# Fetching u and v rows of an expert pick with one indirect DMA from side-by-side tables

## The chip, the cores and the metric

The kernel runs on one core of a Trainium2 chip. A core has a matrix engine (TensorE, PE in the profile; PEld is its weight load), a vector engine (VectorE, DVE), a scalar engine (ScalarE, ACT), GpSimd (POOL), a queue engine (SyncE, SP), and 16 DMA engines that all queues share. The engines run their own instruction streams in order and wait for each other through semaphores. The metric is the device time of one execution in microseconds (us); lower is better.

## The reference

Two blocks follow each other, in float32, on 256 tokens of width 1024. The first is a hybrid mixer (gated linear attention beside a state-space scan) and a feed-forward layer of very many small experts; the second is a retention layer and a stick-breaking attention layer. The change touches the experts alone:

```python
def peer_ffn(h, w_q, sub_keys, u_tab, v_tab):      # T = 256 tokens, 8 heads, 128 x 128 experts
    q = (hb @ w_q).reshape(n, PEER_HEADS, 2, PEER_HALF)
    s = jnp.einsum('nhid,hikd->nhik', q, sub_keys)
    s_top, i_top = lax.top_k(s, PEER_TOPK)                                # 16 of 128, twice per head
    cand = s_top[:, :, 0, :, None] + s_top[:, :, 1, None, :]
    cand_idx = i_top[:, :, 0, :, None] * PEER_N_KEYS + i_top[:, :, 1, None, :]
    best, pos = lax.top_k(cand.reshape(n, PEER_HEADS, PEER_TOPK * PEER_TOPK), PEER_TOPK)
    idx = jnp.take_along_axis(cand_idx.reshape(n, PEER_HEADS, -1), pos, axis=-1)
    w = jax.nn.softmax(best, axis=-1)
    u = jnp.take(u_tab, idx, axis=0)                                      # rows of 1024 floats
    act = jax.nn.gelu(jnp.einsum('nhkd,nd->nhk', u, hb))
    out = jnp.einsum('nhk,nhkd->nd', w * act, jnp.take(v_tab, idx, axis=0))
```

So each token takes 8 x 16 = 128 experts, and for each a row of `u_tab` and a row of `v_tab`, 4096 bytes each.

## The kernel before, in words

Tokens lie on the 128 partitions, in two tiles i = 0, 1. One "pick" m is one expert for each of 128 tokens: m // 16 is the pair n of head and token tile, m % 16 the rank of the expert. There are 256 picks. A pick needs one u row and one v row per partition, 2 x 512 KB.

All weights come as a stream of 512 KB chunks on SP's queue (`load`, L186) into four `raw` buffers. `do_split` (L192) makes of each chunk a high part `whi` (ACT) and a low part `wlo` (DVE), five buffers each; `triple` (L233) multiplies with three matmuls. `XH` and `XL` hold the two parts of the activations. A side job is a generator in `sides`; `side_step` runs a piece of it between the chunks of the stream, so its instructions fall between the chunks' in program order, and `side_all` runs what is left.

The expert stage is the `stream_T` of `peer_w_q` at L1122 (16 chunks, a step after each half chunk) with `scores` after each pair of chunks, and `peer_side` (L1087) beside it. Per pair n, `topk` (L1019) finds 16 indices and weights on DVE. Per pick:

- `gather_u` and `gather_v` (L1056, L1059): one indirect DMA each, issued by POOL at L1052, into one of 8 u buffers or 7 v buffers. It waits for the indices and for the buffer: a u buffer is free after its dot product, a v buffer after its matmuls; two of the v buffers lie where the sub-keys were and wait for the last score matmuls, `st7`.
- `dot` (L1063): on DVE, u times the token's row, summed (L1066); after four of them GELU on ACT (L1070) and the weight on DVE (L1071).
- `expert` (L1075): ACT writes a diagonal matrix with the weights of the pick (L1079); PE multiplies it with the v row in two matmuls of 512 columns into PSUM, which sums over the picks (`mm`, L293). The trace records each of these matmuls as two.

The loop of `peer_side` sets the order: a u gather each step, its dot 6 steps later, v gathers 24 steps behind u at first and 4 at the end, experts 6 picks behind v. After it the sums are added to the residual (L1133), normalised, and the second block begins, whose first five chunks are split before the expert stage ends.

Of the kernel before, what the change touches and what calls it, by code (L numbers as in the profile page):

```python
# [8 lines left out]
F32 = mybir.dt.float32  # L9
F32R = mybir.dt.float32r  # L10
# [11 lines left out]
CH = 1024  # L22
# [2 lines left out]
AHEAD = 4  # L25
XW = 8 * T + 8 * TX
ARENA = 27648
LU, LE = 6, 6
NEG = -3.0e38


# [93 lines left out]
    return chunks  # L125


def build(nc, stream, par, rows, con1, con2, xin, meta, subk, peer_u, peer_v, out, stage=99, debug=None):
    chunks = chunk_plan()
    ctx = ExitStack()  # L130
    with ctx:
        def sb(name, shape, dt=F32):
            return ctx.enter_context(nc.sbuf_tensor(name, shape, dt))

        def sem(name):
            return ctx.enter_context(nc.semaphore(name))

        raw = [sb(f"raw{i}", [128, CH]) for i in range(NR)]
        whi = [sb(f"whi{i}", [128, CH], F32R) for i in range(NS)]
        wlo = [sb(f"wlo{i}", [128, CH], F32R) for i in range(NS)]  # L140
        XH = sb("XH", [128, XW], F32R)
        XL = sb("XL", [128, XW], F32R)
        C1 = sb("C1", [128, NC1])
        PAR = sb("PAR", [128, NPAR])
        SM = sb("SM", [128, 512])
# [36 lines left out]


        loaded, split, used = {}, {}, {}
        state = {"load": 0, "split": 0, "next": 0}

        def load(i):
            if i < len(chunks) and i == state["load"]:
# [2 lines left out]

        def do_split(i):  # L192

            if i < len(chunks) and i == state["split"]:
                state["split"] += 1
                r, h, l = raw[i % NR][:, :], whi[i % NS], wlo[i % NS]
                a = A(lambda e: e.activation(h[:, :], r, ACT.Copy), loaded[i], used.get(i - NS), chain=False)  # L197
                b = V(lambda e: e.tensor_tensor(l[:, :], r, h[:, :].bitcast(F32), ALU.subtract), a, loaded[i], used.get(i - NS),  # L198
                      chain=False)
                split[i] = (a, b)  # L200
                load(i + NR)
# [802 lines left out]
        NU, NV = 8, 7  # L1004
        UB = [place(f"U{j}", 16896 + 1024 * j, 1024) for j in range(NU)]
        VB = [place(f"V{j}", 2048 + 1024 * j, 1024) for j in range(NV)]
        s_u = [sem(f"s_u{j}") for j in range(NU)]
        s_v = [sem(f"s_v{j}") for j in range(NV)]
        iota16 = C1[:, C_IOTA:C_IOTA + 16]
        idx_pt, w_pt, c_pt = {}, {}, {}  # L1010

# [34 lines left out]
        u_free, v_free, u_in, v_in = {}, {}, {}, {}  # L1046

        def gather(buf, table, n, k, s, *after):
            h, i = divmod(n, 2)
            col = IDX[:, i, 16 * h + k:16 * h + k + 1]  # L1050
            dma_count[s.name] = dma_count.get(s.name, 0) + 16
            G(lambda e: e.indirect_dma_start(buf, None, table, bass.IndirectOffsetOnAxis(ap=col, axis=0)).then_inc(s, 16),  # L1052
              idx_pt[n], *after, signal=False, chain=False)
            return (s, dma_count[s.name])

        def gather_u(m):  # L1056
            u_in[m] = gather(UB[m % NU], peer_u, m // 16, m % 16, s_u[m % NU], u_free.get(m - NU), hn)

        def gather_v(m):  # L1059
            v_in[m] = gather(VB[m % NV], peer_v, m // 16, m % 16, s_v[m % NV], v_free.get(m - NV), hn,  # L1060
                             pts["st7"] if m % NV > 4 else None)

        def dot(m):  # L1063
            n, k = divmod(m, 16)
            h, i = divmod(n, 2)
            u_free[m] = V(lambda e: e.tensor_tensor_reduce(UB[m % NU], UB[m % NU], HN[:, i, :], 1.0, 0.0, ALU.mult, ALU.add,  # L1066
                                                           AV[:, i, 16 * h + k:16 * h + k + 1]), u_in[m], chain=False)
            if k % 4 == 3:
                c = slice(16 * h + k - 3, 16 * h + k + 1)
                a = A(lambda e: e.activation(CC[:, i, c], AV[:, i, c], ACT.Gelu_apprx_tanh), u_free[m])  # L1070
                c_pt[m // 4] = V(lambda e: e.tensor_tensor(CC[:, i, c], CC[:, i, c], WT[:, i, c], ALU.mult), a)  # L1071

        dg_free = {}

        def expert(m):  # L1075
            n, k = divmod(m, 16)
            h, i = divmod(n, 2)
            d = DG[:, m % 4, :]
            a = A(lambda e: e.activation(d, ident, ACT.Copy, scale=CC[:, i, 16 * h + k:16 * h + k + 1]), c_pt[m // 4], dg_free.get(m - 4),  # L1079
                  chain=False)  # L1080
            for half in range(2):
                t = mm(ps[2 * i + half][:, :], d, VB[m % NV][:, 512 * half:512 * half + 512], h == 0 and k == 0, h == 7 and k == 15,
                       half == 1, a, v_in[m], bank_free[2 * i + half])
            dg_free[m] = v_free[m] = t
            pts[f"ffn{i}"] = t

        def peer_side():  # L1087


            best = topk(0)  # L1090
            for _ in best:
                yield
            dots = rows_v = sums = t = 0
            while sums < 256:
                n, k = divmod(t, 16)
                if k == 0 and n < 16:
                    for _ in best:
                        pass
                    best = topk(n + 1) if n < 15 else iter(())
                elif k % 3 == 0:  # L1100
                    next(best, None)
                if t < 256:
                    gather_u(t)
                while dots < min(256, t - LU):
                    dot(dots)
                    dots += 1
                lag = max(4, 24 - max(0, t - 24) // 2)
                while rows_v < min(256, t - lag):
                    gather_v(rows_v)
                    rows_v += 1  # L1110
                    if rows_v > LE:
                        expert(sums)
                        sums += 1
                if rows_v == 256 and t >= 256 + LU + 4:
                    while sums < 256:
                        expert(sums)
                        sums += 1
                t += 1
                yield
# [423 lines left out]


# [14 lines left out]
```

## Time and profile before

| what | value |
|---|---|
| median of 3 runs | 1761.43 us (1761.39 to 1766.36) |
| span of the profiled execution, first to last instruction | 1769.4 us; the page gives no other time for it |
| busy share of the span | PE 82%, DVE 62%, ACT 39%, POOL 32% |
| gathers on POOL | 512, the first at 547.2 us, the last at 1301.9 us |
| bytes by the POOL's DMA queue | 268.47 MB of 415.39 MB in all |

Times in the trace are counted from the span's start. A group of instructions is named by the line of the kernel that issued it, its engine, its operation and "out<-in". The tile `AR` is one large allocation in which most small tiles lie, the u and v buffers among them. "Idle before" is time the engine stood still ahead of an instruction, with what ended the wait; "issue" means that it waited for nothing that the profile shows. The DMA share is the mean busy time of the 16 DMA engines, rounded from packets' records, so that it can read a little over 1.

### The profile page before, as it was taken

How to read it: one execution, taken by the hardware profiler on the slowest of the kernel's cores; microseconds unless marked ns; L12 is line 12 of the kernel's file. 1: busy time of each engine (PE TensorE's matmuls, PEld its weight loads, DVE VectorE, ACT ScalarE, POOL GpSimd, SP SyncE). 2: the span in 40 equal slices, each digit the busy share in tenths (PEclk: the TensorE clock that was granted, in tenths of full speed). 3: DMA queues.
4: the chain of work that ended last, by engine and by line, in shares of the span. 5: the costliest groups of instructions: out<-in, count | busy, mean ns of one | idle time of the engine just before them, and what ended most of it. 6: DMA issues, size and time to landing. Idle time of an engine off the chain costs nothing. (4 is left out here: it accounts for less than half of the span.)

```text
span 1769.4 us, 19554 instructions
## 1 busy us (share of the span) xinstructions
PE 1453.9 (82%) x6773; PEld 988.0 (56%) x6773; DVE 1104.8 (62%) x2088; ACT 695.1 (39%) x1195; POOL 573.7 (32%) x516
## 2 busy tenths in 40 slices
PE   6998998998989487867676676777769999799988
PEld 6986786766969222322222222222239778698866
DVE  5864388776568955466666666666448456654554
ACT  5663454346444312211222221122134456566753
POOL 0000000000004677777777777777730000000000
PEclk9998999999989799999999999999989999899989
DMA  6542343334557899999999999999965446455442
GB/s 214 160 133 73 100 150 101 113 119 133 157 165 278 309 353 365 370 348 390 351 378 370 363 359 372 357 357 379 364 233 168 154 149 195 121 176 158 143 123 92
DMA packets 114721, 415.39 MB, mean 235 GB/s; under 512 B 13104, under 2 KB 13104, under 8 KB 114368
## 3 DMA queue, kind: packets, MB, share of 16 engines
q0 software_dynamic: 73728, 268.47, 40.6%
q1 hardware_dynamic: 40896, 145.69, 26.2%
q8 instruction: 54, 0.88, 0.2%
q14 instruction: 43, 0.35, 0.1%
HBM read 413.02 MB, written 1.08 MB: 234 GB/s over the span
## 5 line engine op out<-in xcount | busy, mean ns | idle before, releaser
L293 PE MATMUL ps<-AR 128*128 128x512 f32 (+9 forms) x1912 | 671.3, 487 | 261.3 <-DMA AR<-in_peer_v,AR 157.9
L293 PEld LDWEIGHTS ps<-AR 128*128 128x128 f32 (+4 forms) x1912 | 282.5, 184 | 632.6 <-issue 500.0
L1052 POOL DMA_INDIRECT AR<-in_peer_u,AR x256 | 285.9, 1117 | 638.5 <-DVE SM L1043 546.7
L1066 DVE CUSTOM_DVE_ANT_0 AR<-AR 128x1024 f32<-128x1024 f32 x256 | 310.4, 1223 | 203.0 <-DMA AR<-in_peer_u,AR 188.3
L198 DVE TENSOR_TENSOR wlo<-raw,whi 128x1024 fp32r<-128x1024 f32 x257 | 312.8, 1222 | 172.7 <-ACT whi L197 170.2
L197 ACT ACTIVATE whi<-raw 128x1024 fp32r<-128x1024 f32 x257 | 269.7, 1055 | 131.8 <-PE ps L236 124.8
L1052 POOL DMA_INDIRECT AR<-in_peer_v,AR x256 | 287.6, 1124 | 90.3 <-issue 59.1
L236 PE MATMUL ps<-XH,whi 128*128 128x256 f32 (+1 forms) x1032 | 307.4, 298 | 7.9 <-ACT AR L982 5.1
L236 PE MATMUL ps<-XH,wlo 128*128 128x256 f32 (+1 forms) x1032 | 299.1, 290 | 0.0
L236 PE MATMUL ps<-XL,whi 128*128 128x256 f32 (+1 forms) x1032 | 299.1, 290 | 0.0
L236 PEld LDWEIGHTS ps<-XH,whi 128*128 128x128 f32 x1032 | 202.7, 196 | 26.8 <-issue 19.2
L236 PE MATMUL ps<-whi,XH 128*128 128x512 f32 x512 | 209.1, 408 | 1.6 <-ACT XH L301 1.6
L236 PEld LDWEIGHTS ps<-XL,whi 128*128 128x128 f32 x1032 | 202.9, 197 | 0.1
L236 PEld LDWEIGHTS ps<-XH,wlo 128*128 128x128 f32 x1032 | 202.4, 196 | 0.0
L236 PE MATMUL ps<-wlo,XH 128*128 128x512 f32 x512 | 200.8, 392 | 0.0
L236 PE MATMUL ps<-whi,XL 128*128 128x512 f32 x512 | 200.6, 392 | 0.0
L1079 ACT ACTIVATE AR<-C,AR 128x128 f32<-128x128 f32 x256 | 93.4, 394 | 203.2 <-PE ps L293 97.1
L1070 ACT ACTIVATE AR<-AR 128x4 f32<-128x4 f32 x64 | 13.2, 205 | 385.3 <-DVE AR L1066 234.3
L236 PEld LDWEIGHTS ps<-whi,XH 128*128 128x128 f32 x512 | 96.8, 189 | 26.5 <-issue 5.6
L236 PEld LDWEIGHTS ps<-whi,XL 128*128 128x128 f32 x512 | 96.5, 189 | 21.2
L236 PEld LDWEIGHTS ps<-wlo,XH 128*128 128x128 f32 x512 | 96.8, 189 | 19.1 <-issue 1.0
L296 PE MATMUL ps<-C,AR 128*128 128x128 f32 x219 | 42.0, 319 | 34.7 <-DVE AR L359 14.4
(214 smaller groups left out, 898.7 us busy)
## 6 DMA issues: line engine op xcount, KB each, us to landing
raw<-in_stream SPq DMA_DIRECT2D x257, 512.0 KB
AR<-in_peer_u,AR POOLq DMA_INDIRECT x256
AR<-in_peer_v,AR POOLq DMA_INDIRECT x256
AR<-scr SPq DMA_DIRECT2D x16, 128.0 KB, 4.2
AR<-in_rows SPq DMA_DIRECT2D x4, 512.0 KB
AR<-in_con SPq DMA_DIRECT2D x1, 1280.0 KB, 6.1
AR<-in_xin SPq DMA_DIRECT2D x2, 512.0 KB, 5.0
AR<-in_xin SPq DMA_DIRECT2D x1, 1024.0 KB, 6.0
```

What stands on the lines that cost most here:

```text
L197: a = A(lambda e: e.activation(h[:, :], r, ACT.Copy), loaded[i], used.get(i - NS), chain=False)
L198: b = V(lambda e: e.tensor_tensor(l[:, :], r, h[:, :].bitcast(F32), ALU.subtract), a, loaded[i], used.get(i - NS), chain=False)
L236: tok = PE(lambda e, s=s, m=m, n=n: e.matmul(out_ap, s, m, start=first and n == 0, stop=last and n == 2), *(after if n == 0 else ()), sign ...
L293: return PE(lambda e: e.matmul(out_ap, l, r, start=start, stop=stop, skip_group_check=onto), *after, signal=sig)
L296: return PE(lambda e: e.transpose(out_ap, in_ap, ident), *after, signal=sig)
L1052: G(lambda e: e.indirect_dma_start(buf, None, table, bass.IndirectOffsetOnAxis(ap=col, axis=0)).then_inc(s, 16), idx_pt[n], *after, signal ...
L1066: u_free[m] = V(lambda e: e.tensor_tensor_reduce(UB[m % NU], UB[m % NU], HN[:, i, :], 1.0, 0.0, ALU.mult, ALU.add, AV[:, i, 16 * h + k:16 ...
L1070: a = A(lambda e: e.activation(CC[:, i, c], AV[:, i, c], ACT.Gelu_apprx_tanh), u_free[m])
L1079: a = A(lambda e: e.activation(d, ident, ACT.Copy, scale=CC[:, i, 16 * h + k:16 * h + k + 1]), c_pt[m // 4], dg_free.get(m - 4), chain=False)
```

## The change

The two tables stand side by side in one array `peer_uv` of 2048 columns, so one indirect DMA per pick fetches u and v rows together, 8192 bytes per partition. There are 16 slots of 2048 columns: six in the arena, open from the start; one in the sub-keys' place; and nine in `SLAB`, which is the memory of `whi`, `wlo`, `XH` and `XL`, now one allocation with the old tiles as views in it. These ten open with `st7`. The five slots on `whi` and `wlo` are given to no pick from 234 (`LAST_WIDE`) on, and the chunks behind `peer_w_q` are split from pick 240 on, after the last reader of these slots. A slot is free after the matmuls that read its v half.

The order is written anew: all of `topk(0)` and six gathers at the first step, four steps that issue nothing, then one pick per step. A step issues the dot of its pick, the weighting and the experts of the group that is waiting, GELU when a group is full (groups of 2 picks up to 24, then of 4), every gather for which a slot has been freed in program order, and a piece of the next `topk`. The stream takes one step per chunk in place of two.

```diff
-LU, LE = 6, 6
+LAST_WIDE = 234
+PEER_END = next(n for n, c in enumerate(chunk_plan()) if c[1] == "ret_w_in_2")
-        whi = [sb(f"whi{i}", [128, CH], F32R) for i in range(NS)]   ...
+        SLAB = sb("SLAB", [128, 2 * NS * CH + 2 * XW])
+        whi = [in_slab(f"whi{i}", CH * i, CH) for i in range(NS)]   ...
-            if i < len(chunks) and i == state["split"]:
+            if i < min(len(chunks), state["limit"]) and i == state["split"]:
+                free = (used.get(i - NS), state["fence"])
...
-        UB = [place(f"U{j}", 16896 + 1024 * j, 1024) for j in range(NU)]
-        VB = [place(f"V{j}", 2048 + 1024 * j, 1024) for j in range(NV)]
+        slots = [place(f"UV{j}", at, 2048) for j, at in enumerate((2048, 4096, 16896, 18944, 20992, 23040, 7168))]
+        slots += [SLAB[:, 2048 * j:2048 * j + 2048] for j in range(9)]
...
+        def slot_for(m):
+            names = list(range(6))
+            if "st7" in pts:
+                names += [6] + list(range(12, 16)) + (list(range(7, 12)) if m < LAST_WIDE else [])
+            names = [j for j in names if j not in holds or holds[j] in read]
+            return min(names, key=lambda j: holds.get(j, -1)) if names else None
+        def gather(m):
+            j = slot_for(m)
+            if j is None:
+                return False
+            first = hn if j < 6 else pts["st7"]
+            free = read[holds[j]] if j in holds else first
+            ...
+            G(lambda e: e.indirect_dma_start(slots[j], None, peer_uv, bass.IndirectOffsetOnAxis(ap=col, axis=0)).then_inc(s, 16),
+              idx_pt[m // 16], free, signal=False, chain=False)
...
-            dg_free[m] = v_free[m] = t
+            dg_free[m] = read[m] = t
...
+            for _ in topk(0):
+                pass
+            while m_next < 6 and gather(m_next):
+                m_next += 1
+            ...
+            for m in range(256):
+                dot(m)
+                size = 2 if m < 24 else 4
+                if waiting:
+                    ms = waiting.pop()
+                    weigh(ms)
+                    for x in ms:
+                        expert(x, c_pt[ms[0]])
+                if m % size == size - 1:
+                    ms = list(range(m - size + 1, m + 1))
+                    gelu(ms)
+                    waiting.append(ms)
+                while m_next < 256 and (m_next // 16 in idx_pt) and gather(m_next):
+                    m_next += 1
+                ...
+                if m >= LAST_WIDE + 6 and m % 2 == 0:
+                    ...
+                    if state["split"] < PEER_END + NS:
+                        do_split(state["split"])
+                yield
-        ring.update(banks=(4, 5), steps=2)
+        ring.update(banks=(4, 5), steps=1)
-        "peer_u": np.asarray(inp["peer_u"])[0],
-        "peer_v": np.asarray(inp["peer_v"])[0],
+        "peer_uv": np.concatenate([np.asarray(inp["peer_u"])[0], np.asarray(inp["peer_v"])[0]], axis=1),
```

POOL, before, from the first gather on; what a row waits for stands in brackets (`s_dve`: a dot or indices, `s_pe`: matmuls):

```order
L1052 DMA AR<-in_peer_u,AR 128x1024 [waits s_dve]
L1052 DMA AR<-in_peer_u,AR 128x1024 x7
L1052 DMA AR<-in_peer_u,AR 128x1024 [waits s_dve] x18
L1052 DMA AR<-in_peer_v,AR 128x1024
L1052 DMA AR<-in_peer_u,AR 128x1024 [waits s_dve]
L1052 DMA AR<-in_peer_v,AR 128x1024 x2
```

Eight u gathers need no freed buffer, 18 more wait for dots, then u and v alternate. The same place in the change:

```order
L1077 DMA AR<-in_peer_uv,AR 128x2048 [waits s_dve]
L1077 DMA AR<-in_peer_uv,AR 128x2048 x5
L1077 DMA AR<-in_peer_uv,AR 128x2048 [waits s_pe] x7
L1077 DMA SLAB<-in_peer_uv,AR 128x2048 x3
L1077 DMA SLAB<-in_peer_uv,AR 128x2048 [waits s_dve]
L1077 DMA SLAB<-in_peer_uv,AR 128x2048 x5
```

Six picks go out at once, six more wait for experts on PE, the thirteenth for `st7`, and nine more follow it without a further wait but that for the second pair's indices.

PE, before, at the last scores (the matmuls of 128 columns) and the first experts (those of 512; `s_v0` is the landing in a v buffer, `s_act` the diagonal):

```order
L236 MATMUL ps<-XH,wlo 128x256
L293 MATMUL ps<-AR 128x128 [waits s_act] x2
L293 MATMUL ps<-AR 128x128 x2
L293 MATMUL ps<-AR 128x512 [waits s_v0,s_act]
L293 MATMUL ps<-AR 128x512
```

All experts stand behind the last chunk and the last scores. In the change the first two experts stand here, between the scores of the fifth head and the chunk behind them (`s_uv0` is the landing in slot 0):

```order
L246 MATMUL ps<-XH,wlo_57 128x256
L303 MATMUL ps<-AR 128x128
L303 MATMUL ps<-AR 128x128 [waits s_act]
L303 MATMUL ps<-AR 128x128 x2
L303 MATMUL ps<-AR 128x512 [waits s_uv0,s_act]
L303 MATMUL ps<-AR 128x512
L303 MATMUL ps<-AR 128x512 [waits s_uv1,s_act]
L303 MATMUL ps<-AR 128x512
L246 MATMUL ps<-XH,whi_53 128x256 [waits s_dve]
```

Two more such pairs stand behind the scores of the sixth and seventh head; the others follow the last scores.

## Rows read from the trace of the kernel before

**Rows 1.** The page, busy time: busy us (share of the span) x instructions of each engine.

```profile
PE 1453.9 (82%) x6773; PEld 988.0 (56%) x6773; DVE 1104.8 (62%) x2088; ACT 695.1 (39%) x1195; POOL 573.7 (32%) x516
```

**Rows 2.** The chain of waits, 500 to 1350 us: share of the span by line.

```profile
by line: POOL AR L1052 10.5%; issue 4.7%; PE ps L293 4.6%; DMA AR<-in_peer_u,AR 4.3%; DMA AR<-in_peer_v,AR 3.8%; PE ps L236 2.9%; DVE AR L1066 0.9%; ACT AR L923 0.3%; DVE AR L1015 0.3%; DVE AR L1014 0.2%; DVE AR L1013 0.2%; ACT AR L1079 0.2
```

**Rows 3.** Windows, line 1052 alone: POOL busy (x), PEclk, DMA share, GB/s.

```profile
547.00:601.80 54.80, 33.60 (x26) 0.83 0.90 338
601.80:1304.00 702.20, 539.94 (x486) 0.97 0.97 364
```

**Rows 4.** Line 1052: ns min/median/max, first and last start; idle before, until.

```profile
L1052 POOL DMA_INDIRECT AR<-in_peer_u,AR x256: 937/941/2000, 547.2 to 1293.6; - x128
L1052 POOL DMA_INDIRECT AR<-in_peer_v,AR x256: 935/978/1995, 601.8 to 1301.9; - x128
...
  issue: 126.7, 416
  PE ps L293: 17.6, 52
  DVE AR L1066: 14.5, 6
```

**Rows 5.** Timeline from 853.5 us: start, us, engine, line, operation, out<-in.

```profile
853.88 1.98 PE L293 MATMUL ps<-AR 128*128 128x512 f32 x4 [2.26 <-issue]
...
854.24 1.22 DVE L1066 CUSTOM_DVE_ANT_0 AR<-AR 128x1024 f32<-128x1024 f32 x1
854.41 1.85 POOL L1052 DMA_INDIRECT AR<-in_peer_v,AR  x1 [0.30 <-issue]
...
856.31 0.40 ACT L1079 ACTIVATE AR<-C,AR 128x128 f32<-128x128 f32 x1 [2.18 <-PE ps L293]
856.57 1.34 POOL L1052 DMA_INDIRECT AR<-in_peer_u,AR  x1 [0.30 <-issue]
...
858.22 0.94 POOL L1052 DMA_INDIRECT AR<-in_peer_v,AR  x1 [0.31 <-issue]
```

**Rows 6.** Windows: PE, PEld, DVE, ACT, POOL busy (x), PEclk, DMA share, GB/s.

```profile
720.00:730.00 10.00, 7.86 (x18) 2.98 (x17) 6.16 (x13) 2.78 (x6) 7.87 (x8) 1.00 1.01 407
...
1050.00:1060.00 10.00, 7.50 (x14) 3.05 (x15) 6.14 (x16) 5.48 (x12) 5.83 (x6) 0.83 0.89 321
1060.00:1070.00 10.00, 6.29 (x15) 2.36 (x14) 5.93 (x17) 0.52 (x2) 7.87 (x8) 1.00 0.85 285
...
1100.00:1110.00 10.00, 7.82 (x16) 2.71 (x16) 6.50 (x16) 1.24 (x4) 7.87 (x8) 1.00 1.03 414
...
1250.00:1260.00 10.00, 7.58 (x16) 2.48 (x15) 4.62 (x8) 0.90 (x3) 7.57 (x9) 1.00 1.03 408
```

**Rows 7.** The page, DMA issues: KB each, median us from issue to landing.

```profile
raw<-in_stream SPq DMA_DIRECT2D x257, 512.0 KB
...
AR<-in_xin SPq DMA_DIRECT2D x1, 1024.0 KB, 6.0
AR<-in_subk SPq DMA_DIRECT2D x1, 1024.0 KB, 6.0
```

**Rows 8.** The chain near 1070 us: a gather from its issue to the dot.

```profile
1069.79 6.74 DMA AR<-in_peer_u,AR
```

**Rows 9.** Timeline of PE: the matmuls of three of the eight scores.

```profile
552.57 1.06 PE L293 MATMUL ps<-AR 128*128 128x128 f32 x8
559.22 1.05 PE L293 MATMUL ps<-AR 128*128 128x128 f32 x8
588.80 1.65 PE L293 MATMUL ps<-AR 128*128 128x128 f32 x6 [1.79 <-ACT AR L982]
```

**Rows 10.** The page, costliest groups: busy us, mean ns of one | idle before.

```profile
L198 DVE TENSOR_TENSOR wlo<-raw,whi 128x1024 fp32r<-128x1024 f32 x257 | 312.8, 1222 | 172.7 <-ACT whi L197 170.2
```

**Rows 11.** The end of the stage: the last gather, and the chain behind it.

```profile
1301.91 0.94 POOL L1052 DMA_INDIRECT AR<-in_peer_v,AR  x1 [0.30 <-issue]
...
1311.98 0.70 DVE AR L1133
```

More of the change, by code:

```diff
@@ L125, in chunk_plan, with build @@
     return chunks
-def build(nc, stream, par, rows, con1, con2, xin, meta, subk, peer_u, peer_v, out, stage=99, debug=None):
+PEER_END = next(n for n, c in enumerate(chunk_plan()) if c[1] == "ret_w_in_2")
+def build(nc, stream, par, rows, con1, con2, xin, meta, subk, peer_uv, out, stage=99, debug=None):
     chunks = chunk_plan()
@@ L184, in build @@
         loaded, split, used = {}, {}, {}
-        state = {"load": 0, "split": 0, "next": 0}
+        state = {"load": 0, "split": 0, "next": 0, "limit": PEER_END, "fence": None}
         def load(i):
@@ L1056, in gather_u @@
[L1056 to L1061, printed above, removed]
-        def dot(m):
+        slot_of, holds, uv_in, read = {}, {}, {}, {}
+        dot_pt, gelu_pt, c_pt = {}, {}, {}
+        def slot_for(m):
[4 more added lines that the diff above has]
+            return min(names, key=lambda j: holds.get(j, -1)) if names else None
@@ new lines, in dot, with span, gelu @@
+        def dot(m):
+            h, i = divmod(m // 16, 2)
+            u = slots[slot_of[m]][:, 0:1024]
+            at = 16 * h + m % 16
+            dot_pt[m] = V(lambda e: e.tensor_tensor_reduce(u, u, HN[:, i, :], 1.0, 0.0, ALU.mult, ALU.add, AV[:, i, at:at + 1]),
+                          uv_in[m], chain=False)
+        def span(ms):
+            h, i = divmod(ms[0] // 16, 2)
+            return i, slice(16 * h + ms[0] % 16, 16 * h + ms[-1] % 16 + 1)
+        def gelu(ms):
+            i, c = span(ms)
+            gelu_pt[ms[0]] = A(lambda e: e.activation(CC[:, i, c], AV[:, i, c], ACT.Gelu_apprx_tanh), dot_pt[ms[-1]])
@@ L1068, in dot @@
[L1068 to L1079, printed above, removed]
+            d, v = DG[:, m % 4, :], slots[slot_of[m]][:, 1024:2048]
@@ L1085, in expert @@
+            dg_free[m] = read[m] = t
             pts[f"ffn{i}"] = t
         def peer_side():
-            best = topk(0)
-            for _ in best:
-                yield
[L1093 to L1119, printed above, removed]
@@ L1121, in build @@
-        ring.update(banks=(4, 5), steps=2)
+            for _ in topk(0):
+                pass
+            m_next = 0
+            while m_next < 6 and gather(m_next):
+                m_next += 1
+            yield
+            yield
+            yield
+            yield
+            ahead = topk(1)
+            next(ahead)
+            yield
+            next(ahead)
+            yield
+            n_ahead, waiting = 1, []
+            for m in range(256):
[12 more added lines that the diff above has]
+                    m_next += 1
+                if m < 24 or m % 3 == 0:
+                    h = n_ahead // 2
+                    if n_ahead < 16 and f"s{h}" in pts and n_ahead <= m // 16 + 2 and next(ahead, "end") == "end":
+                        n_ahead += 1
+                        ahead = topk(n_ahead) if n_ahead < 16 else iter(())
+                if m >= LAST_WIDE + 6 and m % 2 == 0:
+                    if state["fence"] is None:
+                        state["fence"] = read[max(x for x, j in slot_of.items() if 7 <= j < 12)]
+                        state["limit"] = len(chunks)
+                    if state["split"] < PEER_END + NS:
+                        do_split(state["split"])
+                yield
@@ L1122, in build @@
+            for ms in waiting:
+                weigh(ms)
+                for x in ms:
+                    expert(x, c_pt[ms[0]])
+            yield
+        ring.update(banks=(4, 5), steps=1)
         stream_T([(0, TX, cons_pq(f)) for f in range(16)], 0, TX, xr)
```

44 lines of the change are left out of this document (24 added, 20 removed).

## The prediction

> **What bounds the kernel now.** I read the page's busy times first. TensorE (PE) is busy 82% of the 1769.4 us, more than any other engine [rows 1], but that is a mean over stages with different limits. The chain of waits from 500 to 1350 us, the stage of the expert gathers, is held longest by GpSimd (POOL) at line 1052, the gather instructions [rows 2]. So the stage is read by itself. From the first v gather at 601.8 us to 1304 us POOL runs 486 gathers in 702.2 us [rows 3]: 1.445 us each, 1.111 busy (539.94 / 486) and 0.334 between. A pick takes two, so 2.89 us. Line 1052 says what the gaps are: 126.7 us in 416 steps is issue, about 0.3 us a time, and only 17.6 and 14.5 us are waits for a buffer that PE or VectorE (DVE) still reads [rows 4]. POOL has nothing to wait for: it is full.
>
> One gather is 0.94 us in the usual case, yet the mean is 1.11. The timeline shows why. The gather at 854.41 takes 1.85 us: a dot product on DVE (854.24, 1.22 us) had 1.05 us left to run when it began; the one at 856.57, with half of a dot left, takes 1.34; the one at 858.22, beside no dot, 0.94 [rows 5]. So a gather that starts under a dot is held until that dot is done. This stretch belongs to POOL and DVE, not to the DMA engines.
>
> The DMA engines look full too, 0.97 of their time at 364 GB/s [rows 3], and that is the disputed point: if they were the limit, halving the instructions would bring nothing. Ten-microsecond windows speak against it [rows 6]. At 1100 us they move 414 GB/s, at 720 us 407, at 1250 us (nine gathers) 408; but when POOL falls back to 5.83 us busy and six gathers (1050 us), this window has 321 and the next 285 GB/s, at a share of only 0.89 and 0.85. The rate follows the supply of gathers. At 414 GB/s a pick (two rows of 4096 B on each of 128 partitions, 1.049 MB) takes 2.53 us, 0.36 us less than POOL needs. PE and DVE have room: in these windows they are busy at most 7.86 and 6.50 of 10 us.
>
> **The change, part by part.** *Gathers.* 512 instructions become 256 that carry the same bytes. Per pick POOL needs 1.111 + 0.334 = 1.45 us in place of 2.89. The trace shows no gather of 8192 B rows. Below, its cost is the present 1.45 us; above, twice the busy part, 2 x 1.111 + 0.334 = 2.56 us. At the low end POOL leaves the chain; at the high end it stands level with DMA and costs some 6 us over the stage. I take the low end, since the number of rows per instruction, 128, stays. With POOL out of the way DMA is next. Its time per pick: 2.53 us at the best 10-us window; not below 2.49, a gain of some 1.5% allowed for the longer rows, as the 1 MB load of `subk` in rows of 8192 B lands no sooner than that of `xin` in rows of 4096 B (6.0 us both [rows 7]); not above 2.80, the present mean brought to a full share (1.049 MB / (364 / 0.97)). I take 2.53, because sixteen buffers remove what made the slow windows.
>
> *Buffers.* Before, a u buffer came back after its dot; now a slot comes back when PE has read the v half, and POOL waits for PE at each gather. Queued behind such a wait are only later gathers. What covers it is depth. From issue to the dot it feeds a gather takes 6.74 us [rows 8]; then the slot waits for its own dot (1.22 us), the rest of its group of four (3 x 2.53), one dot more (2.53), GELU, weighting and the diagonal (about 1, of which the diagonal is 0.40) and up to four experts on PE, 1.98 each [rows 5]. First in its group it waits for all the dots and one expert, last in its group for all the experts: about 21 us in either case. Sixteen slots in 21 us could feed a pick every 1.3 us, the eleven left after pick 234 one every 1.9; both are below 2.53, so DMA's queue stays filled and this wait costs nothing.
>
> *Start.* Only six slots are open until the last score matmuls (`st7`), and the first three pairs of experts now stand between PE's weight chunks. Before, a pair of chunks with its scores takes 6.65 us (552.57 to 559.22) and the scores end at 590.45 after stalls; without them the three last sets would come by about 577 [rows 9]. Six experts add 6 x 1.98 = 11.9 us, so `st7` falls near 589; I take 590, no gain and no loss on PE. By then 12 picks are issued and nearly landed; before, 26 u gathers, 13 picks' bytes, were out by 601.8 [rows 3].
>
> *Stream.* From 590 to the last landing: 6 us for pick 12, then 243 x 2.53 = 615 us. Five weight loads of 0.5 MB [rows 7] are put off from the start of the stage to its end, since their splits wait for pick 240: 2.6 MB / 414 GB/s = 6 us more. Last landing: 590 + 6 + 615 + 6 = 1217. The five splits themselves (1.22 us each on DVE [rows 10]) lie where DVE is idle.
>
> *End.* After the last row: dot, GELU, weighting, diagonal about 2.6 us with the handovers, then four experts, 7.9 us: 10.5, so 1227.5. Before, the last gather is issued at 1301.91 and the addition that reads the experts' sums starts at 1311.98 [rows 11]. Behind that point nothing changes, as the same five chunks are split in advance. Moving `whi`, `wlo`, `XH` and `XL` into one allocation moves no instruction.
>
> **Sum.** 1311.98 - 1227.5 = 84.5 us less. The profiled execution's span is 1769.4, and the page gives nothing around it; it stands 8.0 us above the median of the runs, 1761.43. By its own time: 1685; by the median, **1677 us**. Own range of this case: 2.49 to 2.62 us per pick (10 us less, 22 more) and 6 us either way at the start, 1661 to 1705.
>
> **Rivals.** *DMA is the limit already.* For it: a share of 0.97, and full windows of less than 400 GB/s. Against it: [rows 6]. At 2.80 us per pick the stream takes 680 us, 65 more, saving 19.5: 1742. If memory itself gives this core no more than the mean 364 GB/s, a pick stays at 2.88, the stream takes 700, and the saving is 84.5 - 85: no change, 1762. The Trainium skill (DMA: Bandwidth & Descriptors, "Where 436 GB/s comes from") has such a rule: between HBM and SBUF about 358 GB/s per core bind, not the 435 of the fabric. By that figure a pick takes an estimated 2.93 us and the time would be about 1774. The trace disagrees: 407 to 414 GB/s stand in three of the rows named.
>
> *The six-slot start costs more.* Experts in PE's queue wait for rows that arrive while weight loads share the DMA engines; behind them stand the chunks and so `st7`. Against it: by the order the splits do not stand behind dots that are late, and twelve picks' bytes take only 12 x 2.53 = 30 of the 45 us from the first gather at 547.2 [rows 4] on. If `st7` comes at 620: 30 us less gain, 1707.
>
> *Slower: the slots run out.* Each slot passes DMA, DVE, ACT, DVE, ACT and PE before POOL may refill it, and POOL takes refills in order. It decides once a slot's round takes over 16 x 2.89 = 46 us. Were it 49 (say, in-order waits of DVE and ACT for each other double the steps after landing), a pick would take 3.06 us, the stream 744, 129 more: 1677 + 129 = 1806. Against it: 21 us worked out above, less than half.
>
> **How the numbers follow.** Forecast 0.67; DMA already the limit 0.14 (0.04 of it with no change); late start 0.13; slots 0.06. Range: forecast's own, all of the late start and a part of the 1742 case, 1655 to 1728. About 0.3% (5 us) is what a measurement of this kernel can tell from no change. Faster 0.67 + 0.13 + 0.10 = 0.90; same 0.04; slower 0.06.
>
> **What would show it.** Right: POOL mostly idle in the stage, its gaps ended by PE; 256 gathers of about 1 us (about 2 us if the cost goes by bytes); windows at 400 GB/s and more throughout; the addition after the experts near 1228 us. Wrong: DMA at a full share with 365 to 380 GB/s (first rival); the last scores far behind 590 (second); dots that wait for DMA while the DMA share falls below 0.9 and POOL waits for PE (third).

## The result, and the profile after

The changed kernel takes 1690.34 us (median of 4 runs, 1688.3 to 1692.77) where the kernel before took 1763.34 beside it (4 runs, 1761.39 to 1766.36): a ratio of 0.9585, 95% interval 0.9567 to 0.9603, 73 us less. The prediction said 1677, 1655 to 1728.

The page of the changed kernel, busy times and the gathers' DMA queue; beside [rows 1] only POOL has changed much, from 573.7 us to 298.6.

```profile
PE 1450.9 (86%) x6773; PEld 1014.4 (60%) x6773; DVE 1105.3 (65%) x2094; ACT 691.6 (41%) x1201; POOL 298.6 (18%) x260
...
q0 software_dynamic: 36864, 268.45, 38.4%
```

The chain of waits from 500 to 1240 us, by line. POOL headed it in [rows 2]; now the landing of gathers holds 63%.

```profile
by line: DMA AR<-in_peer_uv,AR 34.6%; DMA SLAB<-in_peer_uv,AR 28.8%; PE ps L303 12.3%; PE ps L246 4.5%; issue 3.1%; DVE SLAB L1086 2.8%; DVE AR L1086 2.7%; ACT AR L1107 1.1%; DVE wlo L208 0.8%; DVE AR L1022 0.6%; DVE AR L1023 0.6%; DVE AR L
```

Line 1077, the gather (columns as in [rows 4]).

```profile
L1077 POOL DMA_INDIRECT SLAB<-in_peer_uv,AR x134: 932/946/1978, 598.1 to 1191.5; - x134
L1077 POOL DMA_INDIRECT AR<-in_peer_uv,AR x122: 932/938/1971, 536.6 to 1206.5; - x122
...
  PE ps L303: 325.0, 171
  issue: 24.0, 75
...
DMA to landing us min/median/max: 5.4/25.8/28.4
```

A gather of 8192 B rows is issued in the same 0.94 us as one of 4096 B, so the low end of that term was right. POOL waits for PE 171 times, 325 us, against 17.6 us in [rows 4]. A gather takes 25.8 us to land (median), against 6.74 from issue to dot for the one in [rows 8]: a queue now stands ahead of the DMA engines.

Windows of the stage (columns as in [rows 6]).

```profile
550.00:560.00 10.00, 8.82 (x75) 8.62 (x73) 8.66 (x21) 5.21 (x9) 0.00 (x0) 1.00 1.02 417
560.00:570.00 10.00, 7.33 (x15) 3.53 (x16) 9.36 (x25) 4.12 (x9) 1.33 (x2) 0.66 0.63 236
570.00:580.00 10.00, 8.84 (x58) 7.21 (x57) 6.43 (x21) 3.56 (x8) 1.15 (x2) 1.00 0.48 198
580.00:590.00 10.00, 8.83 (x61) 7.50 (x61) 5.87 (x16) 2.28 (x7) 1.70 (x2) 1.00 0.57 211
...
690.00:740.00 50.00, 37.78 (x83) 15.67 (x82) 36.90 (x87) 12.56 (x33) 23.95 (x21) 0.97 1.01 421
...
1090.00:1140.00 50.00, 37.15 (x77) 15.11 (x75) 36.16 (x87) 11.69 (x31) 23.81 (x20) 0.92 1.01 421
...
1215.00:1220.00 5.00, 5.00 (x12) 2.21 (x13) 2.08 (x3) 0.65 (x3) 0.00 (x0) 1.00 0.13 53
```

From 640 to 1140 us each window of 50 us reads 421 or 422 GB/s: 1.049 MB / 421 = 2.49 us a pick. Before the last scores the engines are half idle (198 to 236 GB/s): the six slots are full. The last row is the tail, while three more picks land: windows of 1 us read a share of 0.37 from 1215 us and 0.06 to 0.08 from 1216 to 1221 us, about one of 16 engines.

The start: POOL, then the first `topk`, a weight split and the first two dots on DVE, the exponential of that `topk` on ACT, then PE's scores (128x128) and experts (128x512).

```profile
543.93 1.25 POOL L1077 DMA_INDIRECT AR<-in_peer_uv,AR  x1 [0.30 <-issue]
566.73 0.95 POOL L1077 DMA_INDIRECT AR<-in_peer_uv,AR  x1 [21.55 <-PE ps L303]
...
596.90 0.94 POOL L1077 DMA_INDIRECT AR<-in_peer_uv,AR  x1 [3.33 <-PE ps L303]
...
526.26 0.29 DVE L1021 MAX8 AR<-AR 128x8 f32<-128x128 f32 x1 [2.05 <-DVEq L1029]
...
536.60 0.23 DVE L1052 TENSOR_SCALAR AR<-AR,SM 128x16 f32<-128x16 f32 x1
536.74 3.49 DVE L208 TENSOR_TENSOR wlo<-raw,whi 128x1024 fp32r<-128x1024 f32 x3
...
551.72 1.22 DVE L1086 CUSTOM_DVE_ANT_0 AR<-AR 128x1024 f32<-128x1024 f32 x1
...
557.18 1.22 DVE L1086 CUSTOM_DVE_ANT_0 AR<-AR 128x1024 f32<-128x1024 f32 x1
...
533.31 0.31 ACT L1041 ACTIVATE AR<-AR,SM 128x16 f32<-128x16 f32 x1 [5.78 <-DVE SM L1039]
...
524.30 1.06 PE L303 MATMUL ps<-AR 128*128 128x128 f32 x8
...
535.17 1.65 PE L303 MATMUL ps<-AR 128*128 128x128 f32 x6 [3.84 <-ACT AR L992]
...
557.76 1.06 PE L303 MATMUL ps<-AR 128*128 128x128 f32 x8
562.67 6.67 PE L303 MATMUL ps<-AR 128*128 128x512 f32 x8 [3.86 <-ACT AR L1107]
574.93 1.06 PE L303 MATMUL ps<-AR 128*128 128x128 f32 x8
...
577.15 3.70 PE L303 MATMUL ps<-AR 128*128 128x512 f32 x8 [1.17 <-ACT AR L1107]
...
588.66 3.70 PE L303 MATMUL ps<-AR 128*128 128x512 f32 x8 [1.17 <-ACT AR L1107]
...
595.70 0.94 PE L303 MATMUL ps<-AR 128*128 128x128 f32 x6 [0.24 <-ACT AR L992]
```

The gather at 596.90 is the thirteenth, the first that waits for `st7`. Two sets of scores stood 6.65 us apart in [rows 9]; with the first pair of experts between them they are 17.2 us apart (557.76, 574.93), since PE stood 3.86 us for a diagonal and then ran the pair in 6.67, part of it at the lower of its clock levels (1.2 GHz; granted clock 0.66 in the window from 560). The other two pairs take 3.70 us each behind a wait of 1.17. The dots of the first pair have no wait for a landing in front of them (551.72, 557.18): their rows were there, and DVE was late, since splits and pieces of the next `topk` stand ahead of the dots.

Ahead of that, DVE runs the whole first `topk` at one go (526.26 to 536.83). ACT waits 5.78 us for it with the exponential (533.31); behind that stand a weight split and the copy (L992) that the second scores need, so PE stands 3.84 us at 535.17 and then runs at the lower clock level (granted clock 0.50 until 536.8). The third scores come at 544.47, 20.2 us behind the first at 524.30, where it was 13.3 in the kernel before (532.63 to 545.92).

The end, to be read beside [rows 11]:

```profile
1206.54 0.94 POOL L1077 DMA_INDIRECT AR<-in_peer_uv,AR  x1 [8.97 <-PE ps L303]
...
1221.61 1.23 DVE L1086 CUSTOM_DVE_ANT_0 AR<-AR 128x1024 f32<-128x1024 f32 x1 [1.22 <-DMA AR<-in_peer_uv,AR]
...
1223.77 7.13 PE L303 MATMUL ps<-AR 128*128 128x512 f32 x16 [1.81 <-ACT AR L1107]
...
1230.94 1.41 DVE L1177 TENSOR_TENSOR AR<-AR,ps 128x512 f32<-128x512 f32 x2 [4.63 <-PE ps L303]
```

### The profile page after: what moved, and what is told of

Read it like the earlier page. It is cut to its first block, busy times and chain, and to the rows that moved or that the text cites. A ratio compares the mean times of both kernels' runs of the same rounds, so it can differ in the third digit from the quotient of the medians.

```text
span 1689.9 us, 19344 instructions
## 1 busy us (share of the span) xinstructions
PE 1450.9 (86%) x6773; PEld 1014.4 (60%) x6773; DVE 1105.3 (65%) x2094; ACT 691.6 (41%) x1201; POOL 298.6 (18%) x260
## 3 DMA queue, kind: packets, MB, share of 16 engines
q0 software_dynamic: 36864, 268.45, 38.4%
## 4 chain that ended last, share of the span: by engine, by line
PE 47%; DMA 28%; DVE 13%; ACT 8%; issue 3%; POOL 0%; DVEq 0%; ACTq 0%; SPq 0%; POOLq 0%
PE ps L246 33%; DMA AR<-in_peer_uv,AR 15%; DMA SLAB<-in_peer_uv,AR 13%; PE ps L303 12%; DVE wlo L208 3%; ACT whi L207 2%; PE ps L306 1%; DVE SLAB L1086 1%; DVE AR L1086 1%; DVE AR L680 1%; ACT AR L933 1%; ACT AR L1107 0%; ACT AR L678 0%; DMA AR<-in_xin 0%; ACT L333 0%
## 5 line engine op out<-in xcount | busy, mean ns | idle before, releaser
L303 PE MATMUL ps<-AR 128*128 128x512 f32 (+7 forms) x1376 | 406.4, 442 | 116.8 <-ACT AR L1107 71.4
L303 PEld LDWEIGHTS ps<-AR 128*128 128x128 f32 (+3 forms) x1376 | 199.1, 183 | 297.5 <-issue 139.1
L303 PE MATMUL ps<-SLAB,AR 128*128 128x512 f32 x536 | 269.5, 657 | 73.9 <-ACT AR L1107 73.4
L1077 POOL DMA_INDIRECT AR<-in_peer_uv,AR x122 | 137.0, 1123 | 740.6 <-DVE SM L1051 536.1
L303 PEld LDWEIGHTS ps<-SLAB,AR 128*128 128x128 f32 x536 | 111.0, 212 | 234.6 <-issue 135.1
L1086 DVE CUSTOM_DVE_ANT_0 SLAB<-SLAB,AR 128x1024 f32<-128x1024 f32 x134 | 162.8, 1222 | 78.0 <-DMA SLAB<-in_peer_uv,AR 77.4
L1086 DVE CUSTOM_DVE_ANT_0 AR<-AR 128x1024 f32<-128x1024 f32 x122 | 148.1, 1221 | 78.5 <-DMA AR<-in_peer_uv,AR 78.5
L1077 POOL DMA_INDIRECT SLAB<-in_peer_uv,AR x134 | 161.4, 1205 | 168.1 <-PE ps L303 130.9
L1107 ACT ACTIVATE AR<-C,AR 128x128 f32<-128x128 f32 x256 | 83.3, 391 | 160.4 <-DVE AR L1099 148.2
L1095 ACT ACTIVATE AR<-AR 128x4 f32<-128x4 f32 (+1 forms) x70 | 14.3, 205 | 328.0 <-DVE AR L1086 323.9
## 6 DMA issues: line engine op xcount, KB each, us to landing
AR<-in_peer_uv,AR POOLq DMA_INDIRECT x122, 25.8
```

The lines of the kernel that those rows point to most:

```text
L303: return PE(lambda e: e.matmul(out_ap, l, r, start=start, stop=stop, skip_group_check=onto), *after, signal=sig)
L1077: G(lambda e: e.indirect_dma_start(slots[j], None, peer_uv, bass.IndirectOffsetOnAxis(ap=col, axis=0)).then_inc(s, 16), idx_pt[m // 16], f ...
L1086: dot_pt[m] = V(lambda e: e.tensor_tensor_reduce(u, u, HN[:, i, :], 1.0, 0.0, ALU.mult, ALU.add, AV[:, i, at:at + 1]), uv_in[m], chain=False)
L1095: gelu_pt[ms[0]] = A(lambda e: e.activation(CC[:, i, c], AV[:, i, c], ACT.Gelu_apprx_tanh), dot_pt[ms[-1]])
```

## Experiments: what set the pace

**Two gathers into the new slots.**

```diff
-G(lambda e: e.indirect_dma_start(slots[j], None, peer_uv, ...).then_inc(s, 16), ...)
+for at, table in ((0, peer_u), (1024, peer_v)):
+    G(lambda e, ...: e.indirect_dma_start(slots[j][:, at:at + 1024], None, table, ...).then_inc(s, 16), ...)
...
```

> The changed kernel, but each pick's rows are fetched by two indirect DMAs (u rows, v rows, 4096 B each, from separate tables) into the same slot in the same order. Theory (POOL's instructions were the bound, 2.89 us a pick): POOL is full again at about 1.4 us a gather, the stage's pick period returns from 2.49 to 2.8-2.9 us, so 0.3 to 0.4 us x 243 picks = 75 to 100 us over the changed kernel's 1690: 1765 to 1790. First rival (the sixteen slots and the new order gave the gain, not the number of instructions): 1690, POOL waiting for PE. Second rival (the row length gave it: DMA is the limit either way, a little worse with 4096 B): 2.53 to 2.6 us a pick, 1700 to 1717, POOL not full.

Measured: 1789.17 us (5 runs), ratio to the kernel before 1.0156 (1.0132 to 1.018). Slots and order without the joined gather are a loss. Line 1078 there:

```profile
  issue: 146.3, 476
  PE ps L303: 41.6, 24
```

POOL's gathers (567 us on its page) and gaps fill the stage, 2.86 us a pick from the fourteenth pick at 605.0 to the last gather at 1297.9. The first rival falls, and the size is the theory's; the second rival is contradicted by POOL being full.

**Seven slots.**

```diff
-names += [6] + list(range(12, 16)) + (list(range(7, 12)) if m < LAST_WIDE else [])
+names += [6]
...
```

> The changed kernel with seven slots in place of sixteen: the nine in the weights' memory are never used. Theory (a slot's round is about 21 us, and depth is what covers it): seven slots give a pick no sooner than every 3 us, up to 4 with groups of four held together, so the stream takes 243 x (3.0 to 4.0) = 730 to 970 us in place of 605: 1815 to 2055, POOL waiting for PE before nearly every gather and the DMA share well under 0.9. Rival (one DMA per pick alone gives the gain, depth beyond seven is not used): 1690.

Measured: 1983.74 us (one run). Line 1077:

```profile
  PE ps L303: 684.7, 230
...
DMA to landing us min/median/max: 5.3/7.6/19.9
```

27 gathers in 100 us make 3.7 us a pick, inside the forecast. So neither part carries the gain alone: the joined gather with too few slots, and the slots with two gathers, are both slower than the kernel before.

**Half the bytes.**

```diff
-e.indirect_dma_start(slots[j], None, peer_uv, ...)
+e.indirect_dma_start(slots[j][:, 1024:2048], None, peer_v, ...)
...
```

> The changed kernel, fetching only the v half of each pick: 256 gathers as before, each of 512 KB in rows of 4096 B into the same slots in the same order (the u rows are left out, the dot product takes the v row instead, scaled, and the argument of one exponential of the second block is halved). Theory (the bytes are the bound now, 2.49 us a pick for 1.049 MB): the next limit is PE with some 1.8 to 2.0 us a pick, 0.5 to 0.7 x 243 = 120 to 170 us less, 1520 to 1575, DMA share near 0.7 or below. Rival (the slots' round through DVE, ACT and PE sets the pace, not the bytes): about 1690, POOL's waits for PE as long as now. Second rival (POOL's instruction is the bound): POOL full, 1690.

Measured: 1539.06 us (one run), as the theory had it. One window:

```profile
740.00:790.00 50.00, 45.10 (x100) 19.02 (x99) 44.75 (x111) 13.54 (x36) 27.51 (x25) 0.97 0.78 261
```

PE and DVE are 90% busy, DMA has room (a share of 0.78, though 0.7 or less was expected), and a pick takes 1.92 us. In the changed kernel the bytes set the pace; next stand PE and DVE together.

**Short dots in the kernel before.**

```diff
-e.tensor_tensor_reduce(UB[m % NU], UB[m % NU], HN[:, i, :], 1.0, ...)
+e.tensor_tensor_reduce(UB[m % NU][:, 0:128], UB[m % NU][:, 0:128], HN[:, i, 0:128], 1.0, ...)
...
```

> The kernel before the change, with the dot products over the first 128 of 1024 columns only (seven eighths of each dot product are left out, and the argument of one exponential of the second block is halved to keep values finite); the gathers and all else stay. Theory (POOL was full, and a gather that starts under a dot is held until the dot ends): dots of some 0.3 us hold little, gathers go back to 0.94 + 0.33 = 1.27 us, a pick to 2.55 us, level with the DMA engines: 0.34 us x 243 = 80 us less, 1680 to 1700, and 410 GB/s or more with rows of 4096 B. Rival (the DMA engines were at their limit already at a mean of 364 GB/s, or rows of 4096 B can't go faster): 1755 to 1763, unchanged, and POOL's gaps become waits.

Measured: 1737.6 us (one run): 24 us less than before, not 80. Two lines of its page, then two of its windows:

```profile
L1052 POOL DMA_INDIRECT AR<-in_peer_u,AR x256 | 249.2, 974 | 619.5 <-DVE SM L1043 536.9
...
L1052 POOL DMA_INDIRECT AR<-in_peer_v,AR x256 | 246.2, 962 | 157.4 <-issue 71.1
```

```profile
850.00:860.00 10.00, 7.82 (x16) 2.71 (x16) 4.09 (x23) 0.65 (x2) 7.56 (x9) 1.00 1.03 416
...
870.00:880.00 10.00, 6.88 (x11) 2.99 (x12) 3.90 (x19) 2.33 (x7) 5.58 (x6) 0.66 0.82 284
```

The hold is shown: the mean gather falls from 1.11 to 0.97 us when dots are short. The Trainium skill (SBUF — State Buffer, "SBUF: two separate sides") says that the software which writes a gather's descriptors is locked out of a port while some DVE instructions run; this run agrees, as far as shorter dots make shorter gathers (1.11 to 0.97 us). But POOL, now able to give a pick in 2.54 us (2 x 0.97 + 2 x 0.30), gave one in 2.71 (256 v gathers from 581.1 to 1271.9): it stood still ahead of v gathers, 22.8 us for PE and 64.1 us for what the trace does not name, and the rate swung between 416 and 284 GB/s. Most likely the seven v buffers come next, close behind POOL, which no run shows; the prediction had priced depth only for the kernel after.

**Two gathers, sixteen slots, short dots.** The edits of the first experiment and of the short dots together.

> The kernel of the first experiment (two gathers a pick, rows of 4096 B, sixteen slots) with the dot products over the first 128 of 1024 columns (seven eighths of each are left out, and the argument of one exponential of the second block is halved). It parts the three things that the change joins: number of instructions, row length, depth. Theory (POOL's time per pick set the pace, and it was 2.89 us because dots held the gathers; depth is there): gathers at 0.94 + 0.30 us, a pick in 2.49 to 2.55 us, 410 to 421 GB/s with 4096 B rows: 1690 to 1705. Rival (rows of 4096 B give no more than some 370 GB/s with both tables in turn, as before): 1765 to 1790, landings of 20 us and more, POOL waiting for PE.

Measured: 1770.89 us (one run): 2.86 us a pick, no better than with full dots. The theory's number is wrong here. Line 1078, then two windows:

```profile
  PE ps L303: 59.6, 31
  remote: 53.7, 22
```

```profile
850.00:860.00 10.00, 3.64 (x6) 1.39 (x6) 1.69 (x9) 0.40 (x1) 6.17 (x7) 0.80 1.02 406
860.00:870.00 10.00, 8.83 (x15) 3.24 (x14) 4.85 (x27) 2.71 (x9) 5.79 (x7) 0.69 0.86 295
```

POOL is not full (7 gathers in 10 us; 8 would fit): it stood still 59.6 us for PE and 53.7 us for a sender that the trace does not name (`remote`). The rate swings as before, with PE nearly idle in one window and full in the next at a granted clock of 0.69. Rows of 4096 B do go at 406 to 417 GB/s in such windows, but no run of this study held them above 385 in a window of 50 us between 640 and 1190 us.

**A slower POOL with long rows, twice.** Behind each gather from the thirteenth to pick 239 POOL zeroes a piece of a slot that is not used.

```diff
+            if "st7" in pts and m < 240:
+                G(lambda e: e.memset(SLAB[:, 16384:17408], 0.0), pts["st7"])   # second run: 16384:17792
...
```

> The changed kernel (one gather a pick, rows of 8192 B) with fifteen slots, and behind each gather from the thirteenth to pick 239 an instruction on POOL that sets 1024 columns of the sixteenth slot to zero: POOL gets slower, rows and bytes stay. The experiment before ended at 1771 though gathers took 0.94 us and POOL could give a pick in 2.49 us. Theory (POOL needs time to spare: with its time for a pick at the DMA engines' 2.49 us no queue builds up in front of them, and what a late slot costs is never caught up): the zeroing is estimated at about 1 us, like a gather, so POOL needs some 2.4 to 2.7 us a pick, landings fall from 25 to 6-10 us, and the time is 1730 to 1790. Rival (the row length sets the rate: 8192 B rows give 421 GB/s, 4096 B rows some 370): POOL below 2.49 us a pick leaves 1690, and above it the time rises only by the excess times 227 picks.

> As the experiment before, with 1408 columns zeroed in place of 1024. There the zeroing took 0.965 us, POOL needed some 2.2 us a pick and the time stayed at 1687; by 0.94 ns a column it takes 1.33 us now, and POOL needs some 2.55 us a pick, just over the DMA engines' 2.49. Theory (POOL without time to spare builds no queue, and what a late slot costs is never caught up, as with two short-dot gathers at 2.49 us a pick that ended at 1771): landings fall to 6-10 us, mean rate 370 to 400 GB/s, 1725 to 1775. Rival (with rows of 8192 B the rate follows POOL's time alone, and the loss with 4096 B rows was theirs): 2.55 us a pick, 227 x 0.06 = 14 us more than 1687: 1695 to 1710.

Measured: 1687.21 and 1713.79 us (one run each). The second run's page and line 1077, then one of its windows:

```profile
L1077 POOL DMA_INDIRECT AR<-in_peer_uv,AR x130 | 151.7, 1167 | 619.4 <-DVE SM L1051 538.2
...
L1080 POOL MEMSET SLAB<- 128x1408 f32 x228 | 293.8, 1288 | 0.1
...
L1077 POOL DMA_INDIRECT SLAB<-in_peer_uv,AR x126 | 142.7, 1132 | 24.6 <-issue 18.4
```

```profile
DMA to landing us min/median/max: 5.5/8.4/17.5
```

```profile
690.00:740.00 50.00, 37.98 (x77) 15.48 (x76) 36.09 (x81) 11.60 (x30) 47.02 (x37) 0.91 1.00 394
```

POOL needs 1.15 + 1.29 + 0.17 = 2.61 us a pick and a pick takes 2.60 (228 of them from 599.8 to 1189.7 us); (2.60 - 2.49) x 227 = 25 us, and the second run is 26.6 slower than the first, where POOL needed 2.34 (1.20 + 0.97 + 0.17), below 2.49, and the time was that of the changed kernel. As far as two single runs go, POOL's time per pick sets the pace where it is above that of the bytes and not where it is below, and my idea that it needs time to spare is refuted: the queue was down to 8.4 us and nothing more was lost. The times are near those of the rival on record, by which the rate with rows of 8192 B follows POOL's time alone (1690; 1695 to 1710 for 2.55 us, where POOL needed 2.61). Its other half, that the loss with 4096 B rows was due to the rows, these runs cannot show, as they fetch no short rows. That long rows alone make the gain does not fit them: POOL at 2.61 took a part of it back with rows of 8192 B.

What stays open is why two gathers of short rows, with no dot to hold them, stayed at 2.86 us. The price of a short packet is not it. In the packet records of the traces, from 640 to 1140 us, a packet of 4096 B takes 159 ns in the median in all five kernels with such rows, and one of 8192 B 309 ns in the second slower run and 313 in the changed kernel: 16 engines at that pace move 412 GB/s of the one and some 420 of the other, 2% apart. The rest are longer packets. They bring the mean to 171 to 174 ns in the four kernels that fetch all bytes in short rows, and to 326 with long rows in the second slower run, where POOL was the one that held back. So a DMA share near 1 does not show that the DMA engines are the limit: the window above has 394 GB/s at a share of 1.00, the changed kernel 421 at 1.01. Whether the slots came back late in the run with two gathers and short dots, or PE's clock, or something else made its packets long, no run parts.

## Experiments: start and end of the stage

**Eleven slots, weights as early as before.** The five slots on `whi` and `wlo` are not used, and the five chunks behind the stage are loaded at its start.

```diff
-state = {"load": 0, "split": 0, "next": 0, "limit": PEER_END, "fence": None}
+state = {"load": 0, "split": 0, "next": 0, "limit": len(chunks), "fence": None}
-names += [6] + list(range(12, 16)) + (list(range(7, 12)) if m < LAST_WIDE else [])
+names += [6] + list(range(12, 16))
...
```

> The changed kernel with eleven slots: the five on the weights' split buffers are never used, and the five weight chunks behind the stage are loaded and split as early as before the change. Theory (a round of 21 us needs about 9 slots at 2.49 us a pick; the five loads cost DMA time at the end and none at the start, where the DMA engines are half idle between 560 and 600 us): the rate in the stage is unchanged at 421 GB/s, the end comes 5 to 6 us sooner: 1684. Rival (sixteen slots are needed to keep the DMA queues filled): the period rises with 21/11 against 21/16 by as much as the round is longer than thought, 2.6 us or more, 1715 or slower.

Measured: 1688.84 us (5 runs), ratio 0.9579 (0.9558 to 0.96): not to be told from the changed kernel. The rate is nearly the same (421 or 422 GB/s in most windows, 413 and 416 in two; landing 13.4 us): eleven slots do. From the fourteenth gather to the last dot it takes 617.1 us (607.8 to 1224.9), 6.4 less than in the changed kernel (598.1 to 1221.6), as the term for the loads had it; from the first scores (531.13) to the addition (1235.22) it is 704.1 us for 706.6, so some of it went at the start.

**Start three steps earlier; the same with eleven slots and smaller last groups.**

```diff
             yield
-            yield
-            yield
-            yield
             ahead = topk(1)
...
-                size = 2 if m < 24 else 4
+                size = 1 if m >= 254 else 2 if m < 24 or m >= 248 else 4    # second kernel alone
```

> The changed kernel with one edit: three of the four empty steps ahead of the first dot are taken out, so picks begin three steps earlier beside the score chunks. Theory (the six-slot start leaves the DMA engines half idle from 560 to 600 us because the first slots are given back only behind the scores of the fifth, sixth and seventh head): slots come back from about 551 us on, some six more picks are fetched ahead of the last scores, worth up to 6 x 2.49 = 15 us, less the experts' time on PE ahead of the last scores (6 x 1.98 = 12 us later): 1680 to 1687. Rival (the last scores come later by as much as is won): 1690.

> A version meant to beat both: eleven slots with the five weight loads where they were before the change, picks begin three steps earlier beside the score chunks, and the last picks go in groups of two and then one. Theory: the rate stays at 421 GB/s; from the changed kernel's 1690 come off 6 us of late loads, about 7 us of DMA time that is idle between 560 and 600 us, and 4 to 5 us of the last experts, which no longer wait for a group of four: 1672 to 1676. Rival (the earlier picks put more experts ahead of the last scores, so the ten other slots open later and the idle DMA time only moves): 1680 to 1685.

Measured: 1697.73 (ratio 0.9634, 0.9611 to 0.9658) and 1697.82 us (0.9631, 0.9608 to 0.9655), 5 runs each: both some 7 us slower than the changed kernel, against all four expectations. A window and POOL in the first of them:

```profile
590.00:600.00 10.00, 7.76 (x31) 4.58 (x29) 3.98 (x9) 3.45 (x9) 0.94 (x1) 0.83 0.12 52
```

```profile
612.98 0.94 POOL L1077 DMA_INDIRECT AR<-in_peer_uv,AR  x1 [0.46 <-issue]
```

The gather of 612.98 is the first behind `st7`, 92.7 us after the first scores (520.32) where the changed kernel has 72.6 (524.30, 596.90). In those 20 us four picks more were issued (16 for 12), worth 4 x 2.49 = 10 us, and DMA falls to 52 GB/s. On average a pair of experts ahead of the scores delays them by more than the two picks that it frees are worth.

**Start six steps later; the same with eleven slots, early weights and smaller last groups.**

```diff
-            yield    # four of them
+            for _ in range(10):
+                yield
```

> The changed kernel with one edit: the first dot comes six steps later, so that no expert stands ahead of the last scores. Theory: scores end near 578 in place of 597, six picks fewer are out by then (15 us): 1685 to 1687. Rival: the idle DMA time only moves, 1690 to 1695.

> Eleven slots with the five weight loads where they were before the change, the last picks in groups of two and one, and the first dot six steps LATER than in the changed kernel, so that no expert stands ahead of the last scores. Theory (each pair of experts ahead of the scores costs the scores more time than the two picks it frees are worth): scores end near 578 in place of 597; six picks fewer are out by then (6 x 2.49 = 15 us): 4 us won; with 6 us of late loads and 5 us at the end: 1674 to 1678. Rival (six picks ahead of the scores are worth what they cost): 1679 to 1685.

Measured: 1685.89 (0.9579, 0.956 to 0.9598) and 1678.41 us (0.954, 0.952 to 0.956), 5 runs each. The second is the best kernel of the study, its interval below that of the changed kernel, and its time just above the theory's 1678; the first is as forecast, though its interval overlaps. POOL and DVE in the second:

```profile
575.16 0.93 POOL L1077 DMA_INDIRECT AR<-in_peer_uv,AR  x1 [30.23 <-PE ps L303]
...
1218.52 1.41 DVE L1169 TENSOR_TENSOR AR<-AR,ps 128x512 f32<-128x512 f32 x2 [1.32 <-PE ps L303]
```

The first slot behind `st7` is taken 21.7 us earlier, and the addition comes 12.4 us earlier, with the first scores at the same 524.29.

## Why the prediction was right, and where it was off

The work ahead of the stage is the same, yet in the profiled executions its first scores came anywhere from 520.3 to 532.6 us. So I count from them: before from 532.63, after from 524.30. The stage up to the addition then took 779.4 us before and 706.6 after, 72.7 less, which is what the medians say (73.0).

| step | forecast | measured |
|---|---|---|
| first scores to the first gather behind `st7` | 532.6 to 590: 57.4 | 524.3 to 596.9: 72.6 |
| from there to the last landing | 590 to 1217: 627 | 596.9 to 1221.6: 624.7 |
| last landing to the addition | 10.5 | 9.3 |
| sum | 694.9 | 706.6 |

The 11.7 us between the sums are most of the 13 by which 1677 was too low (about 1.9 come from the kernel before, 1763.34 against 1761.43). The start alone missed by 15.2 us; the prediction had allowed 6 either way there. The stream looks right by luck: 10 us less for its picks and some 8 more at its tail cancel.

*POOL.* Right: [rows 3] had it at 2.89 us a pick, the run with two gathers puts it back near that time (2.86), and the two slower POOLs show its time setting the pace once it is above that of the bytes. A gather costs POOL the same 0.94 us with rows of 4096 and of 8192 B.

*DMA next.* Right in kind, and 2.49 in place of 2.53 us, 10 us better over 243 picks. But the evidence was thinner than it read: [rows 6] showed 414 GB/s in single windows of short rows, and no run held that for long with 4096 B rows. What is kept up at 421 GB/s is 8192 B rows. Joining the gathers gives fewer instructions and longer rows at once, and no run has the one without the other at full rate: with POOL's hold gone and the old rows, 1737.6 and 1770.9 were reached, not 1690. The first rival, DMA already at its limit, was in that sense closer than its 0.14 said, though packets of 159 ns speak against its mechanism. For one core alone the Trainium skill has the better rule elsewhere (Perfetto Trace Analysis, "Roofline"): a single active core may pass 358 GB/s and is held by the 16 DMA engines at about 435. The 421 agrees.

*Start.* This is the step that failed: "Six experts add 6 x 1.98 = 11.9 us, so `st7` falls near 589." The late-start kernel, with no expert there, shows what each part costs; its first and its last scores:

```profile
522.37 1.06 PE L303 MATMUL ps<-AR 128*128 128x128 f32 x8
...
573.31 0.94 PE L303 MATMUL ps<-AR 128*128 128x128 f32 x6 [0.24 <-ACT AR L992]
```

Its last scores end 51.9 us after its first begin, those of the changed kernel (595.70, 0.94 long) 72.3 after. So six experts cost 20.4 us, not 11.9. At full clock they run 3 x 3.70 = 11.1 us, near the forecast; what the sum left out is that PE waits for the diagonals (3.86 + 1.17 + 1.17 = 6.2 us) and runs the first pair 3.0 us longer at the lower clock. The diagonal of the first pair waits for its dots and its weights, which stand on DVE behind splits and `topk`. The other 7 us are the first `topk` at one go, 20.2 us in place of 13.3 between the first and the third scores, which was no term of the sum. The second rival named the place, at twice the size (30 us), but not this cause: it had the experts wait for rows that land late, and the rows of the first pair were there.

*End.* Right to 1.2 us. But the last landings came late: the rate alone would have put the last one at 596.9 + 6 + 605 + 6 = 1214, and it came at 1221.6, the last of it with a mean DMA share of 0.13. These 8 us were no term of the sum; what holds the last engine back stays open.

*Slots.* Right that sixteen suffice; eleven do, seven do not. (The round of a slot that is last in its group adds up to 19.4 us from the prediction's own terms, not 21, which changes nothing.)

## What to carry to other kernels

When the issue of small gathers fills an engine, join them, and give the joined gather enough buffers in the same change: here either part alone lost time. Work slipped into an in-order engine's queue ahead of a step that many wait for costs its waits too, not its busy time alone. A rate read in the best window of a starved stage is a hope; ask what row length and supply held it, and for how long. A DMA share near 1 can come with 394 GB/s as well as with 421.

## What was not expected of the hardware

- A gather of 128 rows takes 0.94 us to issue for rows of 4096 and of 8192 B, and a row of 8192 B moves as one packet: 36864 packets in place of 73728 for the same 268 MB.
- About one of 16 DMA engines finishes about 5 us behind the rest (share 0.06 to 0.08 in windows of 1 us from 1216 to 1221 us, while picks still land until 1221.6). The Trainium skill (DMA: Bandwidth & Descriptors, "Latency and other measured facts") names two engines that are usually slower in traces; these windows show one engine's worth of lag, not which engine.
- PE's granted clock in the stage is lower than before (0.92 in the window from 1090 us; [rows 3] have a mean of 0.97), though PE has no less to do there. The stream keeps its 421 GB/s all the same; at the start the lower clock costs time.
